# Branch sums in PSUM, one low half moved to VectorE, and another order at the two ends of the expert stage

## The reference, cut to what matters

```python
# first block: two attention branches, gated and merged
gates  = sigmoid(gate_logits + b_gate)
merged = gates[..., :D_MODEL] * o_a + gates[..., D_MODEL:] * o_b    # o_a, o_b: branch outputs after their projections
x = x + rms_norm(merged @ w_out, g_post_mix)
m = square(relu(rms_norm(x, g_pre_mlp) @ w_up)) @ w_down
...
# second block, last part: every expert is evaluated densely, its weight is zero where it was not chosen
act = gelu(einsum('td,thkd->thk', xb, expert_u[e]))
x   = x + einsum('thk,thkd->td', g * act, expert_v[e])
return rms_norm(x, final_norm_g)                                     # x * rsqrt(mean(x*x) + eps) * final_norm_g
```

## Time and profile before

| | us |
|---|---|
| median of 3 runs | 1335.96 |
| lowest and highest | 1333.66, 1337.6 |
| the profiled execution, its time | 1333.44 |
| the profiled execution, its span | 1331.7 |

### The profile page before, as it was taken

The page is one execution under the profiler, slowest core; times in us unless marked ns, Lnnn a source line. Parts: engine busy times, 40 slices in busy tenths (PEclk is TensorE's granted clock), DMA queues, the critical chain, the costliest instruction groups (busy, mean ns, idle before and its releaser), DMA issues.

```text
span 1331.7 us, 21891 instructions
## 1 busy us (share of the span) xinstructions
PE 1284.4 (96%) x8592; PEld 1169.9 (88%) x8592; DVE 940.0 (71%) x1664; ACT 690.8 (52%) x1135; POOL 33.1 (2%) x27
## 2 busy tenths in 40 slices
PE   7999998999989988999999999999999999999997
PEld 6889978998878777999999999999978888888886
DVE  5766576675446755899999777777767766777675
ACT  5565546654446555344454455555554455445554
POOL 0000031000010000000000000000000000000000
PEclk9999999999999999999999999999999999999999
DMA  7533455656655435567777766565666677666673
GB/s 244 168 115 127 128 173 159 182 184 187 192 174 181 133 108 165 158 195 230 228 220 235 222 189 202 184 203 190 205 241 242 245 245 247 244 244 238 240 241 120
DMA packets 72661, 260.55 MB, mean 196 GB/s; under 512 B 8224, under 2 KB 8864, under 8 KB 72304
## 3 DMA queue, kind: packets, MB, share of 16 engines
q1 hardware_dynamic: 71520, 255.77, 59.0%
q0 software_dynamic: 1040, 3.38, 0.9%
HBM read 240.25 MB, written 18.87 MB: 195 GB/s over the span
## 4 chain that ended last, share of the span: by engine, by line
PE 87%; DVE 5%; ACT 4%; DMA 2%; issue 1%; SPq 0%; DVEq 0%; ACTq 0%
PE ps L937 25%; PE ps L457 14%; PE ps L465 14%; PE ps L467 14%; PE ps L466 14%; PE ps L920 2%; ACT whi L974 1%; PE ps L500 1%; DVE wlo L1402 1%; DVE mg L1660 1%; PE ps L475 1%; DMA X<-in_x_dram 1%; DMA raw<-in_expert_v_dram 1%; PE ps L481 1%; PE ps L873 1%
## 5 line engine op out<-in xcount | busy, mean ns | idle before, releaser
L1402 DVE TENSOR_TENSOR wlo<-raw,whi 128x1024 fp32r<-128x1024 f32 (+2 forms) x410 | 497.7, 1216 | 324.5 <-ACT whi L974 322.2
L974 ACT ACTIVATE whi<-raw 128x1024 fp32r<-128x1024 f32 (+2 forms) x421 | 441.7, 1051 | 439.4 <-PE ps L937 164.1
L465 PE MATMUL ps<-TH,whi 128*128 128x256 f32 x1536 | 441.0, 287 | 2.5 <-DVE TL L1411 1.4
L466 PE MATMUL ps<-TL,whi 128*128 128x256 f32 x1536 | 434.3, 283 | 0.0
L467 PE MATMUL ps<-TH,wlo 128*128 128x256 f32 x1536 | 434.2, 283 | 0.0
L465 PEld LDWEIGHTS ps<-TH,whi 128*128 128x128 f32 x1536 | 294.2, 192 | 3.1 <-issue 3.1
L466 PEld LDWEIGHTS ps<-TL,whi 128*128 128x128 f32 x1536 | 294.4, 192 | 0.0
L467 PEld LDWEIGHTS ps<-TH,wlo 128*128 128x128 f32 x1536 | 294.2, 192 | 0.0
L937 PE MATMUL ps<-whi,TH 128*128 128x512 f32 x512 | 199.5, 390 | 2.2 <-issue 1.5
L937 PE MATMUL ps<-whi,TL 128*128 128x512 f32 x512 | 199.3, 389 | 0.0
L937 PE MATMUL ps<-wlo,TH 128*128 128x512 f32 x512 | 199.3, 389 | 0.0
(11 more groups left out here) (290 smaller groups left out, 1324.6 us busy)
## 6 DMA issues: line engine op xcount, KB each, us to landing
raw<-in_expert_u_dram SPq DMA_DIRECT2D x128, 512.0 KB, 3.8
raw<-in_expert_v_dram SPq DMA_DIRECT2D x128, 512.0 KB, 4.0
raw<-in_w_up_dram SPq DMA_DIRECT2D x32, 512.0 KB, 3.6
raw<-in_w_down_dram SPq DMA_DIRECT2D x32, 512.0 KB, 3.6
acts<-stage SPq DMA_DIRECT2D x32, 512.0 KB, 4.0
stage<-acts SPq DMA_DIRECT2D x30, 512.0 KB, 3.3
raw<-in_w_in_dram SPq DMA_DIRECT2D x20, 512.0 KB, 3.7
raw<-in_w_gate_dram SPq DMA_DIRECT2D x16, 512.0 KB, 3.4
```

The lines of the kernel that those rows point to most:

```text
L465: e.matmul(dst, whi[:, h, sl], xh[:, k, :], start=k == 0, stop=False)
L466: e.matmul(dst, whi[:, h, sl], xl[:, k, :], start=False, stop=False)
L974: e.activation(whi[:, u % NH, 0:n], raw[:, u % NR, 0:n], ACT.Copy).then_inc(*hi(u))
L1402: e.tensor_tensor(wlo[:, u % NH, 0:n], raw[:, u % NR, 0:n], whi[:, u % NH, 0:n].bitcast(F32), ALU.subtract).then_inc(*lo(u))
```

## The change

There are five edits. In the merge, product and sum are written to the chunk's own PSUM bank instead of `mg`, and TensorE waits for the low half of chunk n-4 instead of its sum. DOWN waits for `r30` at its start and for `r31` at its second half. The low half of EV + 1 goes from GpSimd to VectorE. In SP's list the loads of EV + 5 and EV + 6 move ahead, and the return of X moves back. At the end both sums of the first token half come first, the gain is multiplied in before the root is known, and VectorE and ScalarE each do one of the two scalings; ScalarE sends its own half out.

```diff
-LO_POOL = (BR_B + 1, BR_B + 2, BR_B + 3, OUT, OUT + 1, UP, UP + 1, IN2, IN2 + 1, QUERY, EV + 1)
+LO_POOL = (BR_B + 1, BR_B + 2, BR_B + 3, OUT, OUT + 1, UP, UP + 1, IN2, IN2 + 1, QUERY)
...
-        gb4, squares, fin = raw[:, 0, :], raw[:, 1, :], raw[:, 2:4, :]
+        gb4, squares, fin = ACTV[:, 120:124, :].rearrange("p a b -> p (a b)"), raw[:, 1, :], raw[:, 2:4, :]
...
# TensorE: BR_B chunks, h2 turns, DOWN
-                    e.wait_ge(*merge_d.at(f"f{n - 4}"))
+                    e.wait_ge(*merge_d.at(f"low{n - 4}"))
...
-                    e.wait_ge(*merge_d.at(f"f{4 + c}"))
+                    e.wait_ge(*merge_d.at(f"low{4 + c}"))
...
-            e.wait_ge(*relu_a.at("r31"))
             for d in range(2):
+                e.wait_ge(*relu_a.at(("r30", "r31")[d]))
...
# ScalarE: merge and end
-                copy(TH[:, n, :], mg[:, n % 2, 1, :], 0.5).then_inc(*merge_a(n))
+                copy(TH[:, n, :], ps[4 + n % 4][:, 0:256], 0.5).then_inc(*merge_a(n))
...
+                e.wait_ge(*end_d.at(f"r{t}"))
+                e.wait_ge(*end_d.at(f"g{t}0"))
+                copy(fin[:, t, 0:512], fin[:, t, 0:512], r).then_inc(*end_a(f"out{t}0"))
+                e.wait_ge(*end_a.at(f"out{t}0"))
+                e.dma_start(out[t * 128:t * 128 + 128, 0:512], fin[:, t, 0:512]).then_inc(*d_out[2 * t](0))
...
# VectorE: merge
-                e.scalar_tensor_tensor(out=TL[:, n, :], in0=mg[:, n % 2, 1, :], scalar=0.5, in1=TH[:, n, :].bitcast(F32),
+                e.scalar_tensor_tensor(out=TL[:, n, :], in0=ps[4 + n % 4][:, 0:256], scalar=0.5, in1=TH[:, n, :].bitcast(F32),
...
-                m0, m1 = mg[:, n % 2, 0, :], mg[:, n % 2, 1, :]
+                m0, m1 = ps[4 + n % 4][:, 256:512], ps[4 + n % 4][:, 0:256]
...
# VectorE: end (the loop before is shown in full above)
+            def last_sum(t, d):
+                e.wait_ge(*ended.at(2 * t + d))
+                e.tensor_tensor(X[:, t, cols512(d)], X[:, t, cols512(d)], ps[bank4(t, d)][:, :], ALU.add)...
+            def last_gain(t, d):
+                e.wait_ge(*end_d.at(f"x{t}{d}"))
+                e.tensor_tensor(fin[:, t, cols512(d)], X[:, t, cols512(d)], gb4[:, cols512(d)], ALU.mult)...
+            e.wait_ge(*d_back.at(0))
+            e.wait_ge(*d_gb4.at(0))
             for t in range(2):
                 part, v, s, r = end_st[t]
+                last_sum(t, 0)
+                if t == 0:
+                    last_sum(t, 1)
+                e.wait_ge(*end_a.at(f"{t}0"))
+                mean_eps(v, part[:, 0:1], 1024).then_inc(*end_d(f"v{t}"))
+                last_gain(t, 0)
+                if t == 1:
+                    last_sum(t, 1)
+                last_gain(t, 1)
                 e.wait_ge(*end_a.at(f"s{t}"))
                 e.reciprocal(r, s).then_inc(*end_d(f"r{t}"))
+                e.wait_ge(*end_d.at(f"r{t}"))
+                e.wait_ge(*end_d.at(f"g{t}1"))
+                scaled_copy(fin[:, t, 512:1024], fin[:, t, 512:1024], r).then_inc(*end_d(f"out{t}1"))
...
# GpSimd
-            split(EV + 1)
-            e.wait_ge(*lo.at(UNITS - 1))
+            e.wait_ge(*cut_d.at(3))
             e.dma_start(gb4, A["final_norm_g_2"].partition_broadcast(128)).then_inc(*d_gb4(0))
...
# SP
-                if j == 0:
-                    for i in range(30, 32):
-                        e.wait_ge(*d_store[i % 2].at(i))
+                if j < 2:
+                    e.wait_ge(*d_store[j].at(30 + j))
...
+            load(EV + 5)
             store(31)
+            load(EV + 6)
             fetch(0)
-            e.wait_ge(*weighed.at(63))
-            e.dma_start(X[:, :, :], x_kept).then_inc(*d_back(0))
-            for n in range(125):
-                if n % 4 == 0 and 0 < n < 120:
+            for n in range(2, 125):
+                if n % 4 == 0 and n < 120:
                     fetch(n // 4)
                 load(EV + n + 5)
+                if n == 17:
+                    e.wait_ge(*weighed.at(63))
+                    e.dma_start(X[:, :, :], x_kept).then_inc(*d_back(0))
```

More of the change, by code:

```diff
@@ L384, in build @@
         route_a = signal("route_a", ["exp", "turned0", "g_hi"])
-        end_a = signal("end_a", ["00", "01", "s0", "10", "11", "s1"])
+        end_a = signal("end_a", ["00", "01", "s0", "out00", "10", "11", "s1", "out10"])
         low = signal("low", (
@@ L435, in build @@
         end_d = signal("end_d", (
-            "x00 v0 x01 r0 out00 out01 x10 v1 x11 r1 out10 out11").split())
+            "x00 x01 v0 g00 g01 r0 out01 x10 v1 g10 x11 g11 r1 out11").split())
         def tensor_program(e):
@@ L2057, in vector_program @@
             split(EV + 127)
+            def last_sum(t, d):
+                e.wait_ge(*ended.at(2 * t + d))
+                e.tensor_tensor(X[:, t, cols512(d)], X[:, t, cols512(d)], ps[bank4(t, d)][:, :], ALU.add).then_inc(
+                    *end_d(f"x{t}{d}"))
+            def last_gain(t, d):
+                e.wait_ge(*end_d.at(f"x{t}{d}"))
+                e.tensor_tensor(fin[:, t, cols512(d)], X[:, t, cols512(d)], gb4[:, cols512(d)], ALU.mult).then_inc(
+                    *end_d(f"g{t}{d}"))
+            e.wait_ge(*d_back.at(0))
+            e.wait_ge(*d_gb4.at(0))
             for t in range(2):
                 part, v, s, r = end_st[t]
-                for d in range(2):
-                    e.wait_ge(*ended.at(2 * t + d))
-                    if t == 0 and d == 0:
-                        e.wait_ge(*d_back.at(0))
-                    e.tensor_tensor(X[:, t, cols512(d)], X[:, t, cols512(d)], ps[bank4(t, d)][:, :], ALU.add).then_inc(
-                        *end_d(f"x{t}{d}"))
-                    if d == 0:
-                        e.wait_ge(*end_a.at(f"{t}0"))
-                        mean_eps(v, part[:, 0:1], 1024).then_inc(*end_d(f"v{t}"))
+                last_sum(t, 0)
[7 more added lines that the diff above has]
+                last_gain(t, 1)
                 e.wait_ge(*end_a.at(f"s{t}"))
                 e.reciprocal(r, s).then_inc(*end_d(f"r{t}"))
-                if t == 0:
-                    e.wait_ge(*d_gb4.at(0))
-                for d in range(2):
-                    e.wait_ge(*end_d.at(f"r{t}"))
-                    e.scalar_tensor_tensor(out=fin[:, t, cols512(d)], in0=X[:, t, cols512(d)], scalar=r, in1=gb4[:, cols512(d)],
-                                           op0=ALU.mult, op1=ALU.mult).then_inc(*end_d(f"out{t}{d}"))
+                e.wait_ge(*end_d.at(f"r{t}"))
+                e.wait_ge(*end_d.at(f"g{t}1"))
+                scaled_copy(fin[:, t, 512:1024], fin[:, t, 512:1024], r).then_inc(*end_d(f"out{t}1"))
         def pool_program(e):
@@ L2156, in sync_program @@
                     store(n // 4 - 1)
+            load(EV + 5)
             store(31)
+            load(EV + 6)
             fetch(0)
-            e.wait_ge(*weighed.at(63))
-            e.dma_start(X[:, :, :], x_kept).then_inc(*d_back(0))
-            for n in range(125):
-                if n % 4 == 0 and 0 < n < 120:
+            for n in range(2, 125):
+                if n % 4 == 0 and n < 120:
                     fetch(n // 4)
                 load(EV + n + 5)
+                if n == 17:
+                    e.wait_ge(*weighed.at(63))
+                    e.dma_start(X[:, :, :], x_kept).then_inc(*d_back(0))
             for t in range(2):
-                for d in range(2):
-                    e.wait_ge(*end_d.at(f"out{t}{d}"))
-                    e.dma_start(out[t * 128:t * 128 + 128, cols512(d)], fin[:, t, cols512(d)]).then_inc(*d_out[2 * t + d](0))
+                e.wait_ge(*end_d.at(f"out{t}1"))
+                e.dma_start(out[t * 128:t * 128 + 128, 512:1024], fin[:, t, 512:1024]).then_inc(*d_out[2 * t + 1](0))
             for i in range(4):
```

## The result

| | before | after |
|---|---|---|
| median of the runs, us | 1337.64 (1333.52 to 1342.23, 11 runs) | 1329.3 (1327.16 to 1332.68, 11 runs) |
| ratio after / before | | 0.9949, interval 0.9936 to 0.9962 |
| span of the profiled execution, us | 1331.7 | 1325.5 |

The account below looks back on a forecast made before the run. TensorE, holding 87% of the chain of waits at full clock, was taken as the bound, so only its stops and the end could give time: 3.8 + 0.7 + 0.2 + 1.0 + 1.6 = 7.3 us, 1335.96 to 1328.7 us, range 1325.2 to 1333.0.

Parts of the forecast that it names:

- The merge: BR_B to OUT: with product and sum in PSUM, GpSimd no longer holds VectorE's sums; 3.8 us less.
- three stops: Start of OUT: TensorE's waits for low halves would go, giving 1.28, 1.2 and 1.2 us.
- last stop: Start of OUT: TensorE's third wait for a low half, at 188.19, would go, giving 1.2 us at least.
- UP to DOWN: Between UP and DOWN: first DOWN matmul starts 0.12 us behind the last of UP, not 0.75; 0.7 us less.
- restart: First step of DOWN: TensorE's slow step after a stop, 0.31 instead of 0.23 us, would go; 0.1 us.
- EV + 1: Ahead of EV: VectorE makes this low half, the lock goes but the low half takes its place; 0.2 us less.
- EV + 5: In EV: its load, issued ahead of store, fetch and X, lands in time and TensorE's stop goes; 1.0 us less.
- The end: After the last matmul: reordered sums, gains and scalings finish earlier, last two transfers leave together; 1.6 us less.
- (a): In the merge: GpSimd still holds the sum, so the merge gives nothing; 1332.5 us, chance 0.11.
- (b): In the merge: VectorE's PSUM writes are dear and make it slower, at worst 1344.0 us; chance 0.03.
- (c): In the loads: X or `gb4` collides with other transfers, bringing a 1.0 us stop back; 1329.7 us, chance 0.07.
- (d): At the end: no gain, ScalarE's transfer starts late or its scaling waits behind its own issue; 1330.3 us, chance 0.09.

Follow-up runs that it names:

- two experiments on the operands: Changed kernel with only the product back in SBUF, 1333.55 us; changed kernel with only the sum written to SBUF, 1329.57 us (one execution each).
- the merge alone: Kernel before with only the merge's edits (product and sum in PSUM, TensorE waits for the low half): 1332.68 us, ratio 0.9974.
- take-first kernel: Changed kernel with VectorE's low half of EV + 1 behind the first cut: 1326.56 us, ratio 0.9927; once more 1328.63 us, ratio 0.9943.
- X early: Changed kernel with the return of X right behind the first fetch again, EV + 5's load still ahead of both: 1332.62 us (one execution).

## Why the prediction was right, and where its sizes were off

The forecast, 1328.7 us, is 0.6 us from what was measured, and part of that closeness is luck. It was counted from a median before of 1335.96 us out of three runs, which came to 1337.64 us out of eleven, and the median after stands at the upper edge of the lower of two groups of runs. The fairer comparison is the gain: 7.3 us in the sum, 6.8 us by the ratio, 6.2 us in the profiles. In the profiles, the parts of the sum came to 7.1 us, too little for the merge and too much for the end; UP took back 1.33 us that the sum did not have, and the start of the program gave 0.38 us by chance.

- **The merge** was 4.16 us, worked out as 3.8. The one price that the trace did not hold, a write to PSUM, was 0.428 us, the value taken. The three stops went. The two experiments on the operands show the mechanism, that two SBUF inputs are held, and the merge alone shows the size in the same 32.43 us. Of the other 0.36 us, 0.24 lie in BR_B, where TensorE's steps at 175.89 and 176.13 took 0.24 and 0.22 us instead of 0.11: chunk 6 waited for the sum of chunk 2, which was held until 176.08. The prediction did not see this wait. The other 0.12 us are the last stop, 1.32 us in the trace where 1.2 were taken.
- **UP to DOWN** was 0.63 us for 0.7. The 0.1 us of restart in the 0.7 were there as well, but lie in the next row of the table: the first step of DOWN took 0.34 us before and 0.23 us after.
- **EV + 1** was 0.22 us for 0.2, and for the reason given: the held cut went, and the low half took its place ahead of the first take. The take-first kernel shows the 1.43 us that this order costs.
- **EV + 5** was 1.03 us for 1.0. The working left open which of the things ahead of the load counts. X early shows that moving the loads was enough.
- **The end** was 1.07 us for 1.6, the term of the sum that was mis-sized. The working on the engines held nearly: the last issue came 1.56 us earlier for 1.68. The step that failed is the one behind it, that the last two transfers leaving together instead of 0.66 us apart would cost about 0.1 us. They cost 0.49 us, since the last landing stands 2.7 us behind the first of the two issues, whether the second follows 0.67, 0.38 or 0.24 us later. That first issue came 5.01 us behind the start of the last matmul before and 3.88 us after, 1.13 us earlier, and this is nearly all that the end gave.
- **The clock in front of UP** is not in the prediction at all. It took 1.33 us back in the profile.

Of the rivals, (a), the sum still held, is out by the sums of 0.43 us inside GpSimd's instructions. (b), dear writes to PSUM, needed 1.67 us in the mean for a sum. (c), colliding transfers, needed a stop in EV, and none is left. (d), an end that gives nothing, is out by the 1.07 us, and neither of its reasons was seen: ScalarE's scaling started with VectorE's (1321.69), and its transfer left right behind it (1322.45). What was lost at the end was lost to the pair of transfers.

## What to carry to other kernels

When a short operation of VectorE with two SBUF inputs is long wherever GpSimd works, put its partial result in PSUM, so that no operation has two SBUF inputs: that gave back 4.2 us here, where taking the work from GpSimd gave nothing, because VectorE and ScalarE then waited for each other. Look at every operation of the chain, since with the sum alone in SBUF the low halves behind it were held instead (34.21 us for the stage). When work moves to an engine to end a hold, look at what stands behind it there (1.4 us, and a placement behind the first cut brings it back in the profile), and before moving a big transfer ask whether the small one's place in the queue is the whole cause. At the end of a kernel that sends its last pieces close together, count from the first of them: here, getting the last one out earlier gave nothing. And the clock behind an idle stretch wants a margin of its own in any sum of freed stops, here 1.3 to 2.0 us.
